# Neighbourhood attention with the softmax rows divided by their sums before they are transposed

## What is computed

```python
for l in range(DEPTH_2):
    h = rmsnorm(x, norm_g[l])
    proj = h @ w_in[l]
    ...
    out_a = neighborhood_attention(q_a, k_a, v_a, na_rpb[l])
    ...
    out_b = diff_attention(q_b, k_b, v_b, t5_table, lam, lam_init, subln_g[l])
    y = jnp.concatenate([out_a * jax.nn.silu(g_a), out_b * jax.nn.silu(g_b)], axis=-1)
    x = x + y @ w_out[l]
return rmsnorm(x, final_g)
```

## Time and profile before

| | us |
|---|---|
| median of 3 runs | 941.02 |
| lowest, highest of the runs | 941.01, 1134.88 |
| the profiled execution, its own time | 941.23 |
| its span, first to last instruction | 939.4 |
| of that, TensorE busy | 906.4 |

### The profile page before, as it was taken

One profiled execution on the slowest core, in us unless ns is written; L12 is line 12 of the kernel. 1 busy time (PEld: TensorE's weight loads), 2 busy tenths in 40 slices (PEclk: granted clock), 3 DMA queues, 4 the chain that ended last, 5 costly groups with the idle time before them and its releaser, 6 DMA issues.

```text
span 939.4 us, 14917 instructions
## 1 busy us (share of the span) xinstructions
PE 906.4 (96%) x5861; PEld 715.3 (76%) x5861; DVE 587.7 (63%) x1200; ACT 450.7 (48%) x962; POOL 70.3 (7%) x89
## 2 busy tenths in 40 slices
PE   3999999999999999999999999999999999999996
PEld 1689888865667788887888877888887788887785
DVE  5899798998886472438862448344255965335733
ACT  4734223666784243436925348233434863436631
POOL 1001130006300010000010000000000010000002
PEclk9999999999999999999999999999999999999999
DMA  9735636266000232332304224122243222333203
GB/s 380 312 109 125 181 136 180 102 209 239 1 2 23 90 129 90 112 101 76 111 8 150 90 90 134 43 90 90 90 155 92 62 91 89 94 100 118 72 0 90
DMA packets 34647, 104.71 MB, mean 111 GB/s; under 512 B 14929, under 2 KB 14929, under 8 KB 32146
## 3 DMA queue, kind: packets, MB, share of 16 engines
q1 hardware_dynamic: 28098, 85.77, 27.5%
q0 software_dynamic: 3824, 15.73, 5.2%
q10 hardware_dynamic: 2656, 2.26, 1.0%
HBM read 98.37 MB, written 4.19 MB: 109 GB/s over the span
## 4 chain that ended last, share of the span: by engine, by line
PE 88%; DVE 6%; ACT 2%; issue 2%; DMA 1%; SPq 0%; POOL 0%; POOLq 0%; DVEq 0%; ACTq 0%
PE bank L1023 81%; PE bank L1384 2%; PE bank L1522 2%; DMA ring<-in_w_ada 1%; PE bank L1364 1%; DVE ring L2083 1%; PE bank L1440 1%; DVE arena L1651 0%; DVE ring L2282 0%; ACT ring L834 0%; PE bank L1430 0%; ACT arena L715 0%; DVE soft L2115 0%; ACT w_hi L882 0%; DVE soft L2093 0%
## 5 line engine op out<-in xcount | busy, mean ns | idle before, releaser
L2138 DVE TENSOR_TENSOR w_lo<-ring,w_hi 128x1024 fp32r<-128x1024 f32 x80 | 97.8, 1225 | 114.6 <-ACT w_hi L882 111.5
L1023 PE MATMUL bank<-w_hi,hT_hi 128*128 128x512 f32 x320 | 125.3, 392 | 1.3 <-issue 1.0
L1023 PE MATMUL bank<-hT_hi,w_hi 128*128 128x512 f32 x320 | 126.3, 395 | 0.0
L1023 PE MATMUL bank<-hT_lo,w_hi 128*128 128x512 f32 x320 | 124.6, 389 | 0.0
L1023 PE MATMUL bank<-hT_hi,w_lo 128*128 128x512 f32 x320 | 124.6, 389 | 0.0
L1023 PE MATMUL bank<-w_lo,hT_hi 128*128 128x512 f32 x320 | 124.6, 389 | 0.0
L1023 PE MATMUL bank<-w_hi,hT_lo 128*128 128x512 f32 x320 | 124.5, 389 | 0.0
L882 ACT ACTIVATE w_hi<-ring 128x1024 fp32r<-128x1024 f32 x80 | 84.4, 1058 | 11.6 <-PE bank L1023 11.4
L1023 PEld LDWEIGHTS bank<-w_hi,hT_hi 128*128 128x128 f32 x320 | 60.1, 188 | 14.7 <-issue 2.6
L1023 PEld LDWEIGHTS bank<-hT_hi,w_hi 128*128 128x128 f32 x320 | 60.1, 188 | 14.0 <-issue 0.7
L1023 PEld LDWEIGHTS bank<-hT_lo,w_hi 128*128 128x128 f32 x320 | 60.1, 188 | 12.8
(11 more groups left out here) (323 smaller groups left out, 1814.1 us busy)
## 6 DMA issues: line engine op xcount, KB each, us to landing
ring<-in_w_units SPq DMA_DIRECT2D x80, 512.0 KB, 3.6
ring<-in_w_ada SPq DMA_DIRECT2D x4, 2048.0 KB, 10.2
bias_ring<-in_na_bias POOLq DMA_DIRECT2D x8, 1024.0 KB, 5.5
ring<-in_w_out SPq DMA_DIRECT2D x2, 2048.0 KB, 8.7
bias_ring<-in_t_bias POOLq DMA_DIRECT2D x8, 448.0 KB, 3.8
x_t<-in_x SPq DMA_DIRECT2D x4, 512.0 KB, 5.9
arena<-in_w_ada SPq DMA_DIRECT2D x1, 2048.0 KB, 20.3
arena<-in_w_ada SPq DMA_DIRECT2D x2, 1024.0 KB, 23.2
```

The source lines that it names most:

```text
L1023: return pe.matmul(out, lhsT, rhs, start=first, stop=last)
L2138: dve.tensor_tensor(w_lo[:, u % 4], raw_w[:, u % 4], w_hi[:, u % 4].bitcast(fp32), SUB).then_inc(S["w_split"], 1)
```

## The change

The rows of a unit are divided by their sums in `prob2`, ahead of the transposes. Head 0 of a unit is scaled by POOL (`na_scale`, a tensor_tensor with the inverse sum broadcast), head 1 by DVE (a tensor_scalar in `na_inverse`). The two matmuls that spread the inverse sums, and the multiplication by them in `na_out`, go. `na_turn` lags by three steps behind the score and not by two (`NA_LAG`), and so do `na_move` and, by one more, `na_weigh`; `na_out`, `na_hi` and `na_lo` come two steps later in DVE's loop. The first four steps of output tile 0 move into PE's loop at j = 16, and those of tile 1 in front of the wait for the last `na_lo`. POOL's loads of bias are woven in among its scalings. A semaphore is renamed, and a wait in the first block goes with it.

```diff
+            def na_scale(l, m):
+                M = N_NA * l + m
+                pool.wait_ge(S["na_rinv"], 2 * M + 1)
+                p = prob2[:, m % 8, 0:KW]
+                pool.tensor_tensor(p, p, rinv[:, 2 * M % 16:2 * M % 16 + 1].to_broadcast([P, KW]), MUL).then_inc(S["na_scaled"], 1)
...
-                for n in range(at_ + DAH + 2, min(at_ + LOADS + 2, LOADS * LAYERS)):
-                    load_bias(n)
+                for m in range(N_NA):
+                    if m % NT == NT - 1 and at_ + DAH + 2 + m // NT < LOADS * LAYERS:
+                        load_bias(at_ + DAH + 2 + m // NT)
+                    na_scale(l, m)
...
-                        na_move(l, 0)
-                        for j in range(N_EARLY, N_NA + 2):
-                            na_move(l, j - 2)
+                        for j in range(N_EARLY, N_NA + NA_LAG):
+                            na_move(l, j - NA_LAG)
...
                 for e in range(2):
-                    pe.wait_ge(S["na_exp"], 2 * M + e + 1)
+                    if e == 0:
+                        pe.wait_ge(S["na_scaled"], M + 1)
+                    else:
+                        pe.wait_ge(S["na_rinv"], 2 * M + 2)
...
-                pe.wait_ge(S["na_rinv"], M + 1)
-                for e in range(2):
-                    hf = slice(e * HD, (e + 1) * HD)
-                    r = (2 * M + e) % 16
-                    ins = mm(out[hf, KW + m % 2 * P:KW + (m % 2 + 1) * P], rinv[:, r:r + 1].to_broadcast([P, HD]), ident, False, m % 2 == 1)
...
+                        for j in range(N_EARLY, N_NA + NA_LAG + 1):
                             if j < N_NA:
                                 na_score(l, j)
+                            if j <= N_EARLY + 1:
+                                pe.wait_ge(S["proj_evac"], pt2(l, 8) - 1 + j - N_EARLY)
+                            if j < N_NA + NA_LAG:
+                                na_turn(l, j - NA_LAG)
+                            if j > N_EARLY:
+                                na_weigh(l, j - NA_LAG - 1)
+                            if j == N_NA:
+                                out_rows(0, 6, range(0, 4))
+                        out_rows(1, 7, range(0, 4))
...
                 M = N_NA * l + m
                 dve.wait_ge(S["na_exp"], 2 * M + 2)
-                if M >= 8:
-                    dve.wait_ge(S["na_weighed"], M - 7)
                 r = slice(2 * M % 16, 2 * M % 16 + 2)
                 dve.reciprocal(rinv[:, r], ssum[:, r]).then_inc(S["na_rinv"], 1)
+                dve.wait_ge(S["na_rinv"], 2 * M + 1)
+                p = prob2[:, m % 8, KW:2 * KW]
+                dve.tensor_scalar(p, p, rinv[:, 2 * M % 16 + 1:2 * M % 16 + 2], None, MUL).then_inc(S["na_rinv"], 1)
...
-                tt(y, o[:, 256:512], y, MUL)
                 dve.tensor_tensor(y, o[:, 0:256], y, MUL).then_inc(S["na_out"], 1)
```

More of the change, by code:

```diff
@@ L400, in build @@
         MIX_LAG = 2
+        NA_LAG = 3
         GLU_BANKS = [7, 2, 3, 4]
@@ L1450, in tile_T, with tile_tok @@
                 return ins
-            def tile_tok(out, l, g, i, order=range(KD), between=None):
+            def tile_tok(out, l, g, i, order=range(KD), between=None, steps=range(KD)):
                 tok = slice(i * P, (i + 1) * P)
-                for m, k in enumerate(order):
+                for m in steps:
+                    k = order[m]
                     u = first_unit(l, g) + m // 2
@@ L1606, in _, with out_rows @@
                     else:
-                        for j in range(N_EARLY, N_NA + 3):
+                        def out_rows(t, b, steps):
+                            pe.wait_ge(S["na_taken"], 2 * (N_NA * (l + 1) - 1))
+                            pe.wait_ge(S["mixT_lo"], 4 * (l + 1))
+                            return tile_tok(bank[b], l, 8, t, OUT_ORDER, None, steps)
+                        for j in range(N_EARLY, N_NA + NA_LAG + 1):
                             if j < N_NA:
                                 na_score(l, j)
[L1610 to L1616, removed]
+                            if j <= N_EARLY + 1:
[7 more added lines that the diff above has]
+                        out_rows(1, 7, range(0, 4))
                 pe.wait_ge(S["na_taken"], 2 * N_NA * (l + 1))
[L1618 to L1623, removed]
+                pe.wait_ge(S["na_lo"], N_NA // 2 * (l + 1))
+                for t in range(2):
+                    out_rows(t, 6 + t, range(4, KD)).then_inc(S["wo_done"], 1)
+                for t in range(2, 8):
                     c, i = divmod(t, 4)
-                    if t >= 2:
-                        pe.wait_ge(S["x_ready"], 8 * (l + 1) + t - 1)
+                    pe.wait_ge(S["x_ready"], 8 * (l + 1) + t - 1)
                     hook = None
-                    if t == 0:
-                        hook = na_ready
-                    elif t == 7 and l + 1 < LAYERS:
+                    if t == 7 and l + 1 < LAYERS:
                         hook = lambda: (rows_T(l + 1, 0), rows_T(l + 1, 1))
@@ L2004, in _ @@
             kc = kc_sb[0:64, 2 * HD:3 * HD]
-            dve.tensor_copy(kc, bank[5][0:64, 0:HD]).then_inc(S["kc_used"], 1)
-            dve.wait_ge(S["kc_used"], 1)
+            settle(dve.tensor_copy(kc, bank[5][0:64, 0:HD]))
             dve.tensor_tensor_reduce(kc_sb[0:64, 0:HD], kc, kc, 1.0, 0.0, MUL, ADD, ss[0:64, 48:49]).then_inc(S["k_stats"], 1)
@@ L2342, in _ @@
                                 na_inverse(l, j - 1)
-                            if j >= 5 and j % 2:
-                                na_out(l, (j - 5) // 2)
                             if j >= 7 and j % 2:
-                                na_lo(l, (j - 7) // 2)
-                            if j >= 5 and j % 2:
-                                na_hi(l, (j - 5) // 2)
+                                na_out(l, (j - 7) // 2)
+                            if j >= 9 and j % 2:
+                                na_lo(l, (j - 9) // 2)
+                            if j >= 7 and j % 2:
+                                na_hi(l, (j - 7) // 2)
                             if j - MIX_LAG in MIX_AT:
@@ L2352, in _ @@
                         na_inverse(l, N_NA - 1)
-                        for g in range(N_NA // 2 - 2, N_NA // 2):
+                        for g in range(N_NA // 2 - 3, N_NA // 2):
                             na_out(l, g)
```

7 lines of the change are left out of this document (3 added, 4 removed).

## The result

| | before | after |
|---|---|---|
| median of the runs, us | 941.17 (4 runs) | 948.43 (4 runs, 948.29 to 948.75) |
| profiled execution, span, us | 939.4 | 946.5 |
| ratio, 95% interval | | 1.0074 [1.0062, 1.0086] |

(One of the four runs of before, 1134.88 us, stands 20% above the other three, for a reason that no trace here shows, and is left out of the ratio.) The kernel is slower by 0.74%: inside 2%, on the slower side, 2.4 us over the 946.0 forecast and inside the range. The forecast was right in size and in the engine that it names. One step of it was wrong, and the profile shows which.

A forecast was written before the change was run, and what follows sets the result against it. PE bounds the kernel before (busy 906.4 of 939.4 us); the bound passes to DVE, whose collisions with POOL add 2.4 us a layer. Two layers: 941.2 + 4.8 = 946.0 us, range 938.5 to 955.

The forecast's parts named there:

- What bounds it: Neighbourhood attention loop: the bound passes from PE to DVE (3.80 us a pair of steps), losing nearly all of 10.2 us.
- the rival without a collision: DVE and POOL don't collide in a way that counts; steps 1.76 (even) and 2.04 (odd), 940.5 us; chance 0.20.
- a collision which makes it slower: DVE and POOL exclude each other at every unit after the reciprocal: +2.4 us a layer; chance 0.40.
- The order within it: After the reciprocal DVE's tensor_scalar goes first, then POOL holds for 0.75 us and DVE's next two-input instruction waits.
- POOL comes first: Rival: POOL's scaling precedes the tensor_scalar, which waits; steps 2.32, 2.60, 1.73; +4.3 us a layer, 949.8 us; chance 0.20.
- The seven steps: DVE from the take of unit 8 to that of unit 15: 15.5 us against 13.1 before, +2.4 a layer.
- my even step: DVE's mixing even step: `mixT_lo` waits for POOL until 1.95 us after the take; next take at 2.43.
- my odd step and step 14: DVE: at odd steps `na_lo` waits for POOL, next take at 2.36 us; step 14 has no collision, 1.17.
- POOL's instruction: POOL's tensor_tensor scaling head 0, 256 columns: 0.75 us, between 0.65 from below and 1.3 from above.
- PE's saving: Dropping the two spreading matmuls takes 0.32 us a unit off PE, 10.2 us over 32 units, leaving a step of 1.62.
- The loop's end: Moved output matmuls cover the last scalings and the last out, hi and lo, as before; cost nothing.
- The bias: Bias load for units 8 to 11: unit 8 can't be taken sooner than 8.1 us after the load's start.

The follow-up runs named there:

- Experiment 2: Changed kernel without POOL's scaling: head 0 is left undivided, DVE still scales head 1; 940.83 us, ratio 0.9995.
- experiment 1: Changed kernel with POOL's scaling released by the end of DVE's tensor_scalar instead of by the reciprocal; 942.63 us, ratio 1.0016.
- experiment 5: Changed kernel with both heads scaled by POOL (two tensor_tensors), DVE keeping only the reciprocal; 937.94 us, ratio 0.9966.
- experiment 3: Changed kernel without either scaling: only the reciprocal is left and nothing is divided; 938.04 us, ratio 0.9965.
- experiment 7: Changed kernel with POOL released by the end of DVE's tensor_scalar, and reciprocal and tensor_scalar last in DVE's step; 939.97 us, ratio 0.9987.

## Why the prediction was right, and where it was wrong

**What bounds it: right.** PE's step lost its matmuls, and DVE's steps set the pace. Experiment 2 confirms both numbers on which this rests, 1.76 and 2.02 measured for 1.76 and 2.04, and that alone eats the gain: 940.83 against the 940.5 of the rival without a collision.

**That there is a collision which makes it slower: right, shown by 7.6 us.** By the rule of the Trainium skill that the prediction quoted ("SBUF — State Buffer", section "Who interferes with whom") a DVE instruction with two SBUF inputs contends too; the trace of experiment 1 agrees, with 0.72 for 0.41 at `na_lo`. The same rule of the Trainium skill has the one that starts first make the other wait; by the starts that the trace gives, that did not hold at the tensor_scalar (0.04 to 0.11 us ahead, and held back 32 times of 32).

**The order within it: wrong.** The step that failed is "the tensor_scalar runs from 0.89 and lets go at about 1.2, POOL holds from 1.2 to 1.95". In the trace POOL holds from 0.92 to 1.53 after the take (576.79 to 577.40 for a take at 575.87), and the tensor_scalar lets its successor start at 1.60, at all 32 units. That is the rival "POOL comes first", to which I gave 0.20. With the measured 0.61 in place of its 0.75 its steps of 2.32, 2.60 and 1.73 become 2.18, 2.46 and 1.59; measured are 2.21, 2.48 and 1.61 in the mean. My argument against it was that DVE waits only 0.04 us after the reciprocal. The margin was true and decided nothing. The prediction names this very sign, "if the tensor_scalar is the stretched one (POOL first)", as one by which the forecast is wrong; that 946 stood near 948.4 is in part luck. The seven steps came to 15.67 against my 15.5 because two errors met: my even step was too long (with DVE first `mixT_lo` would not have waited at all, as experiment 1 shows), and my odd step and step 14 too short: 3 x 0.22 too much against 3 x 0.12 and 0.44 too little. **A sum that comes out right doesn't vouch for its terms; the groups do.**

**Terms that were mis-sized.**

- POOL's instruction: 0.75, measured 0.612. It lies under half of the 1.306 of the 512 form, so the line through two sizes did not reach down to 256 columns, and the end taken "from below" was too high.
- PE's saving: 0.32 a unit, measured 0.22. With the spreading matmuls in place the next group started 0.49 after the weighing; without them it starts 0.59 after it. So the whole of PE's saving was 32 x 0.22 = 7.0 us rather than 10.2, and PE's step 1.73 rather than 1.62. Of this 3.3 us became time in experiment 5.
- The loop's end, which I cost at nothing: +1.28 us in layer 0 and +1.35 in layer 1. 1.11 of it stands in a row: the weighing at 591.48 waits for the `out` at 590.92, which stands behind a stretched tensor_scalar (590.19 to 591.00). The moved output steps, which were to cover such a wait, stand behind that weighing in PE's list. This is what made 948.4 of 946: the seven steps gave 2.55 + 2.39 = 4.9 for the 4.8 forecast, the ends 2.6 more, the parts ahead of unit 8 0.5 less.
- The bias, by which unit 8 "can't be taken sooner" than 8.1 us after the load's start: where a take of unit 8 waited for its bias, it came between 6.8 and 8.9 us after the load's start (both in experiment 3, layers 0 and 1; 7.7 and 7.0 in experiment 5, 8.3 and 7.9 in experiment 2). In layer 1 of the kernel before it came after 7.96 and did not wait. A wait of 0.26 on a transfer gives its length in that execution, not a bound.
- The tensor_scalar alone: 0.36, measured 0.354.

**The sign in PE's busy time** was right, its size not: 6.0 less and 13.1 more idle, against 10 and 15.

What stays open: what decides who gets the resource. The lead by the trace's starts does not. A DVE tensor_scalar lost with leads of 0.04 to 0.11 (the changed kernel), `mixT_lo` won with 0.16 to 0.18 (experiment 1), but in the kernel before a tensor_tensor of DVE won with 0.06, and in experiment 7 `na_lo`, at 1.06 us for 0.41, lost with 0.14:

```profile
588.59 1.06 DVE L2268 TENSOR_TENSOR hT_lo<-y,hT_hi 128x256 fp32r<-128x256 f32 x1
...
588.73 0.63 POOL L565 TENSOR_TENSOR ring<-ring,small 128x256 f32<-128x256 f32 x1
```

The lag of three and the moved output steps were never run alone. Whether a bias load cut in two pieces would let unit 8 start earlier wasn't tried.

## What to carry to other kernels

Before work is moved to GpSimd to relieve the vector engine, list which instructions of both touch SBUF in a way that excludes the other, and by what each is released: when one semaphore releases both, reckon with the vector engine waiting out all of GpSimd's instruction, as it did here 32 times of 32, and either let GpSimd start after the last such instruction of the step (experiment 7) or give it the whole of the work (experiment 5), never half of it at the same moment. And before a gain is booked on the bounding engine, take away the work altogether in one run: here that run gained 3 us of the 10 that the rows seemed to promise.

## What the runs showed of the hardware

- A start that the trace puts 0.04 to 0.11 us ahead of GpSimd's did not win the resource that the two share, in 32 cases of 32: the tensor_scalar took 0.80 to 0.90 us beside POOL's 0.61 and ended 0.15 to 0.16 after it. For another pair of instructions a lead of 0.06 did win, so the lead alone is not the rule.
- An instruction that is held back costs less than the wait plus its own time: with POOL ending at 576.34 in experiment 1, `na_lo`, 0.41 alone, ended 0.28 later; the tensor_scalar, 0.35 alone, 0.16 later (changed kernel). Some of the time that it takes alone has thus passed during the wait; which part, no row shows.
- A conversion from SBUF to SBUF with one input (the CAST of `na_hi`) is excluded too: 556 ns beside POOL in experiment 5, 284 in the changed kernel. The take and `na_out`, with one input in PSUM, are not. Both are seen in DVE's timeline of experiment 5:

```profile
574.48 0.42 DVE L2239 CUSTOM_DVE_ANT_0 ring<-bank,bias_ring 128x256 f32<-128x256 f32 x1
...
575.24 0.40 DVE L2253 TENSOR_TENSOR y<-bank,y 128x256 f32<-128x256 f32 x1
...
575.90 0.70 DVE L2258 CAST hT_hi<-y 128x256 fp32r<-128x256 f32 x1
```

  while POOL's timeline has three of its instructions from 574.07 to 576.45:

```profile
574.07 2.38 POOL L566 TENSOR_TENSOR ring<-ring,small 128x256 f32<-128x256 f32 x3 [0.94 <-DVE small L2247]
```

- Four matmuls taken out of a dense stretch of PE, 0.32 us from their start to the next group's, shortened it by 0.22: the group ahead of them then takes 0.10 longer to the start of its successor.
